# Two paddings resized: the distance between TensorE's moving and stationary operands goes from 64 to 96 bytes modulo 512

## The reference

```python
def block(xb):
    q = (xb @ w_query).reshape(PEER_BLOCK, PEER_HEADS, 2, PEER_HALF)
    s = jnp.einsum('mhpd,hpnd->mhpn', q, sub_keys)
    ...                                     # top 16 of 16,384 experts per head
    g = jax.nn.softmax(top, axis=-1)
    act = jax.nn.gelu(jnp.einsum('mhkd,md->mhk', expert_u[idx], xb))
    w = (g * act).astype(xb.dtype)
    return jnp.einsum('mhk,mhkd->md', w, expert_v[idx])
```

## Time and profile before

| | |
|---|---|
| median of three executions | 2159.57 us (2153.75 to 2161.00) |
| the profiled execution's own time | 2152.7 us |
| its span, first to last instruction | 2150.9 us |
| TensorE matmul busy | 2085.3 us (97%), 18,062 instructions |
| TensorE weight load busy | 1981.3 us (92%), 18,062 instructions |
| VectorE | 1432.5 us (67%) |
| ScalarE | 1086.7 us (51%) |
| GpSimd | 486.6 us (23%) |
| mean DMA rate | 165 GB/s |
| mean granted TensorE clock | 0.984 of full |
| chain of work that ended last | PE 87%, DVE 4%, issue 4%, ACT 2%, DMA 2% |

### The profile page before, as it was taken

The page is one execution under the profiler, slowest core; times in us unless marked ns, Lnnn a source line. Parts: engine busy times, 40 slices in busy tenths (PEclk is TensorE's granted clock), DMA queues, the critical chain, the costliest instruction groups (busy, mean ns, idle before and its releaser), DMA issues.

```text
span 2150.9 us, 42650 instructions
## 1 busy us (share of the span) xinstructions
PE 2085.3 (97%) x18062; PEld 1981.3 (92%) x18062; DVE 1432.5 (67%) x2724; ACT 1086.7 (51%) x1881; POOL 486.6 (23%) x230
## 2 busy tenths in 40 slices
PE   7999999999999999999889999999999999999999
PEld 5977999999998789999778899999999999999999
DVE  4445378787785667666663666589388897666666
ACT  5333253232235456446433455555677776555564
POOL 1201100000012120002211441288766662000000
PEclk9999999999998999999999999999999999999999
DMA  7345255466663355764221245565544445555664
GB/s 274 111 138 186 86 180 177 161 225 242 217 231 121 124 180 168 246 197 140 79 79 60 69 138 171 170 190 191 170 145 144 148 147 177 195 188 196 196 193 151
DMA packets 97854, 354.90 MB, mean 165 GB/s; under 512 B 10752, under 2 KB 11776, under 8 KB 97408
## 3 DMA queue, kind: packets, MB, share of 16 engines
q1 hardware_dynamic: 97664, 352.18, 49.0%
HBM read 351.09 MB, written 1.05 MB: 164 GB/s over the span
## 4 chain that ended last, share of the span: by engine, by line
PE 87%; DVE 4%; issue 4%; ACT 2%; DMA 2%; POOL 2%; SPq 0%; POOLq 0%; ACTq 0%; DVEq 0%
PE ps L79 82%; PE ps L84 3%; PE ps L106 1%; POOL TL L113 1%; DVE TL L113 1%; DMA RAW<-in_wada 1%; ACT SQ L154 1%; ACT TH L157 1%; DMA AW<-in_wada 0%; DMA RAW<-in_wdn 0%; ACT Hh L157 0%; POOL SM L113 0%; POOL ACC L113 0%; DVE SQ L113 0%; DVE ps L113 0%
## 5 line engine op out<-in xcount | busy, mean ns | idle before, releaser
L157 ACT ACTIVATE TH<-RAW 128x1024 fp32r<-128x1024 f32 (+1 forms) x515 | 539.7, 1049 | 282.5 <-PE ps L79 255.9
L113 DVE TENSOR_TENSOR TL<-RAW,TH 128x1024 fp32r<-128x1024 f32 (+1 forms) x339 | 417.4, 1231 | 237.0 <-ACT TH L157 236.7
L113 POOL TENSOR_TENSOR TL<-RAW,TH 128x1024 fp32r<-128x1024 f32 x176 | 423.6, 2409 | 492.1 <-ACT TH L157 462.9
L79 PE MATMUL ps<-Hh,TL 128*128 128x256 f32 x1920 | 448.4, 286 | 9.4 <-DVE TL L113 4.3
L79 PE MATMUL ps<-Hl,TH 128*128 128x256 f32 x1920 | 437.0, 280 | 0.4 <-DVE Hl L113 0.4
L79 PE MATMUL ps<-Hh,TH 128*128 128x256 f32 x1920 | 437.0, 280 | 0.0
L79 PE MATMUL ps<-HXh,TL 128*128 128x256 f32 x1314 | 365.8, 283 | 4.3 <-POOL TL L113 2.5
L79 PE MATMUL ps<-HXh,TH 128*128 128x256 f32 x1314 | 360.9, 279 | 0.0
L79 PE MATMUL ps<-HXl,TH 128*128 128x256 f32 x1314 | 360.1, 278 | 0.0
L79 PEld LDWEIGHTS ps<-Hh,TL 128*128 128x128 f32 x1920 | 319.7, 190 | 35.3 <-issue 19.4
L79 PEld LDWEIGHTS ps<-Hh,TH 128*128 128x128 f32 x1920 | 320.1, 190 | 0.7 <-issue 0.5
(11 more groups left out here) (338 smaller groups left out, 3113.3 us busy)
## 6 DMA issues: line engine op xcount, KB each, us to landing
RAW<-in_ut SPq DMA_DIRECT2D x128, 512.0 KB, 3.3
RAW<-in_v SPq DMA_DIRECT2D x128, 512.0 KB, 3.4
RAW<-in_wup SPq DMA_DIRECT2D x88, 512.0 KB, 4.3
AV<-in_wada SPq DMA_DIRECT2D x80, 512.0 KB, 3.8
RAW<-in_win SPq DMA_DIRECT2D x74, 512.0 KB, 3.6
RAW<-in_wada SPq DMA_DIRECT2D x56, 512.0 KB, 3.8
RAW<-in_wdn SPq DMA_DIRECT2D x32, 512.0 KB, 4.3
RAW<-in_wout SPq DMA_DIRECT2D x24, 512.0 KB, 3.7
```

What stands on the lines that cost most here:

```text
L79: return self.e.matmul(out, lhs, rhs, start=first, stop=last, skip_group_check=skip)
L113: return DRY if self.e is None else self.e.tensor_tensor(out, a, b, op)
L157: return DRY if self.e is None else self.e.activation(out, a, ACT.Copy, **kw)
```

## The change

PAD0 shrinks by 8 elements, 32 bytes: everything behind it starts 32 bytes sooner. HXh, HXl, Hh, Hl, MID, MIX, MG, G and all others behind PAD0 move from 448 to 416 modulo 512. PAD2 grows by 16 elements, 64 bytes: W, and the three tensors T behind it, start 64 - 32 = 32 bytes later, W at 96 modulo 512 where it was at 64. RAW, TH and TL stay where they are. No instruction, wait, order or size changes.

```diff
@@ -446,7 +446,7 @@
     RAW = sb("RAW", NRAW * TILE)
     TH = sb("TH", NSPLIT * TILE, F32R)
     TL = sb("TL", NSPLIT * TILE, F32R)
-    sb("PAD0", 112)
+    sb("PAD0", 104)
     HXh = sb("HXh", 2048, F32R)
     HXl = sb("HXl", 2048, F32R)
     XX = sb("XX", 2048)
@@ -558,7 +558,7 @@
-    sb("PAD2", 32, at=late)
+    sb("PAD2", 48, at=late)
     WT = sb("W", 1536, F32R, late)
```

## The result

The changed kernel takes 2205.95 us (median of four executions, 2202.18 to 2209.22) against 2159.80 us (four, 2153.75 to 2161.00): a ratio of 1.0229, interval 1.0210 to 1.0249. It is 46 us slower. The prediction was wrong: its likeliest case was no difference, and the result lies above its range of 2138 to 2200 us, at the price that the slower rival had for all runs together, 2204 us.

A forecast was written before the change was run, and what follows sets the result against it. TensorE's matmuls, their number times their pace, were taken to bound the kernel. Both paddings and the other engines were priced at 0 us, so 2152.7 us stayed 2152.7 us profiled, median 2159.6 us, range 2138 to 2200 us.

The forecast's parts named there:

- its likeliest case: Whole kernel: the change makes no difference, median stays 2159.6 us, own range 2153 to 2166 us; chance 0.38.
- the slower rival: At each run's restart, greater distance makes the longer pace common: likeliest 2182 us, all runs 2204 us; chance 0.36.
- What bounds the kernel: TensorE's chain: some 14,334 matmuls times their pace set the time; 1 ns of pace is worth 14.3 us.
- Two paces at one distance, kept by each run: Matmuls at 64 bytes: 113.3 or about 117.6 ns, each run keeping the one it began with.
- The price of zero: Matmuls of all stages: the distance costs 0 us, taken from weight loads at 111.3 to 111.8 ns whatever the distance.
- The bounds: Every stage: at worst all shorter pace becomes the longer, at best the longer goes and the shorter falls to the load's.
- The likeliest price of half: Slower case with half of the shorter pace lost: +22 us, 2182 us.
- The faster rival: Stages before the last lose the longer pace: some -14 us, 2146 us, or 2124 us at 111.5 ns; chance 0.26.
- The rule on the read ports: TensorE's SBUF connection: independent read ports for moving operand and weight load, so addresses can't matter; same sum of 0 us.
- The other engines and the transfers: VectorE, ScalarE, GpSimd and DMAs on moved tensors: cost nothing, hidden by TensorE's chain.
- The scatter between executions: Spread of 7.25 us over three executions: would be 1700 matmuls taking the other pace, only argued.

The follow-up runs named there:

- e3: Kernel before with 32 bytes of padding ahead of TH, all operands 32 bytes later, distances of 64 bytes kept: 2156.08 us against 2156.20 us, 1.0003.
- e8: Kernel before without the halved matmuls in tiles 1 and 30 of the expert-up and expert-down stages: 2166.06 us, single execution.
- e1: Kernel before with PAD0 shrunk as in the change but W kept at 64 modulo 512 (PAD2 40): 2189.98 us against 2156.20 us, 1.0158.
- e9: Changed kernel without the halved matmuls in tiles 1 and 30: 2200.69 us, single execution.
- e2: Kernel before with PAD2 at 40 and PAD0 unchanged, so W alone moves to 96 modulo 512: 2182.08 us against 2156.20 us, 1.0132.

## Why the prediction was wrong

**What bounds the kernel** was right. The pace of the matmuls sets the time: at 1 ns for 14.3 us, the 46 us are 3.2 ns on average, and the chain shows them as nothing but matmuls.

**Two paces at one distance, kept by each run** was right, and e3 and e8 showed it by experiment: the halved matmuls change the pace within one execution, and without the halved matmuls the last stage stays at 117.7 ns from its first tile to its last.

**The price of zero is the step that failed.** It was taken from weight loads beside a moving operand of one or 128 columns, as the only rows in which the distance differed. They turned out to be rows that don't react. RAW over G went from 64 to 96 bytes apart with the change (RAW moves at 0 and G is stationary, so by the definition above from 448 to 416), and its sixteen loads take 1.86 us after as before:

```profile
1393.89 1.86 PEld L79 LDWEIGHTS ps<-RAW,G 128*128 128x128 f32 x16 [1.37 <-DVE ADA L113]
```

In the same execution the matmuls of 256 columns lost 4 to 7 ns: those before the last stage went from a mean of 114.7 ns to one of 118.0 ns at the full clock, some 38 us for 11,274 of them, and those of the last stage from 113.3 to 120.0 ns, 20.3 us. These two are what the sum had at zero; the 6 us by the clock and the scatter between executions lie between them and the 46 us of the medians. That a load beside a short moving operand has time to spare is the likely reason, and only argued; what is measured is that those loads do not react and these matmuls do. The prediction said that these rows cover only such cases, and used them all the same as the value to take. The better reading stood in the earlier trace rows: beside 256 moving columns the pace was 2 or 6 ns above that of the load alone, by how a run began, so a shift of one stream against the other was likely to act, and only its sign was open.

**The bounds.** The upper bound of every stage was the longer pace seen. The stages before the last kept to it nearly (mostly 117.3 to 118.7 ns, in part 120.0). All of their shorter pace was priced at 44 - 12.9 = 31 us; the trace lost 29.2 us, but only with the clock's 6 us on its side, and e1 lost 35.9 us (1833.1 against 1797.2 us). The last stage didn't: it took a third value, 120.0 ns, and lost 20.3 us where 12.9 had been the most. A bound from the two values at one distance was no bound for another distance; over all distances 113.3 to 123.3 ns were measured.

**The rivals.** The slower one was the right mechanism in part. It said that the greater distance makes the longer pace the common one, and that the halved matmuls need not work after a shift; e9 shows that they even work the other way at 96 bytes, by 2.7 ns. But it isn't the same two paces in another share: each distance has values of its own, and the longer pace of 64 bytes doesn't occur at 96. It should also have been the likeliest. The sentence that three times as much was there to lose as to win was the decisive one, since 64 bytes was the fastest value of all those tried, and it weighed too little beside the zero. The likeliest price of half (2182 us) was under the measured one, and the range's end at 2200 us left out just the case that came. The faster rival has nothing behind it: no kernel tried had fewer matmuls above the shorter pace than the kernel before.

**The rule on the read ports.** The Trainium skill ("TensorE: Matmul & The Clock Gate", Part 2) has the moving operand and the weight load on independent read ports. By that rule no padding could act. The trace disagrees: e1, e2 and e3 differ in nothing but starts, and the last stage has 113.3, 120.0 and 113.3 ns.

**The other engines and the transfers** at nothing was right: e3 moved all tensors but RAW, and the time stayed within 0.2%.

**The scatter between executions** was put down to matmuls that take the other pace. The record speaks for the granted clock instead: of the executions of the kernel before that were run beside the experiments, the three under 2152 us had a mean clock of 0.984 to 0.986, the six above 2159 us one of 0.980 to 0.982. A difference of 0.004 in the mean is 17 us more at the lower level, worth some 8 us by the 118 and 213 ns above. That is a correlation over 21 executions, and no run tests it.

**What stays open.** Why 64 bytes is good, and what collides, if anything does. The runs show that the pace follows the relative start of the two streams, with the values of 0 and 256 bytes and of 64 and 320 alike. They don't show where in the memory or in the engine the time is lost, nor whether the load or the moving operand is the one that waits. All these matmuls of a stage have the same distance, so it is also not parted whether the matmul's own load counts or the next one's, which runs beside it.

## What to carry to other kernels

When weight loads and matmuls both run nearly all of the time, the start addresses of the two operands are a setting of the kernel: here they were worth 3% from the best to the worst, with not one instruction changed. Try the distance between the operands in steps over 256 bytes, each stage by itself, and read the pace in a stretch that holds one kind of matmul, where a step of 4 ns stands out in a single execution; after every change of the layout look again at anything that was put in to steer how a run begins. And a cost may be taken from a neighbouring row only if that row is under the same load: here the rows of loads beside short moving operands did not react to the distance, and those beside long ones did.

## What the runs showed of the hardware that was not expected

- The pace of a float32r matmul of 256 columns with its own weight load took 113.3, 116.6, 117.3, 117.8, 118.3, 118.7, 120.0 or more ns, up to 123.3, by the distance of the two operands alone or by the distance and a start off a multiple of 32 bytes.
- At one distance several paces are stable, and a run keeps the one it began with: at 64 bytes 113.3 and 117.8 ns, at 96 bytes 117.3, 118.7 and 120.0 ns. A few halved matmuls in tile 1 of the last stage, and again in tile 30, decided over 350 us.
- A run doesn't have one interval but often a figure that repeats over five matmuls or so, as 120, 117, 115, 118, 117 ns at 96 bytes and 119, 115, 118, 121, 120 ns at 128.
